# Attention scores in split precision: three one-pass products for a pair of heads in the two row halves

## The reference

```python
# gqa: each query block of 128 sees the key blocks n-1, n, n+1
scores = jnp.einsum("bnqhgd,bnkhd->bnhgqk", qb, kw).astype(jnp.float32) * (d ** -0.5)
# na: rows of a 16 x 64 grid, a window of 8 rows x 16 columns, learned bias
scores = jnp.einsum("brqhd,brikhd->brhqik", qg, kg).astype(jnp.float32) * (d ** -0.5)
# dif: causal, two maps j of a head, bias slope_h * (k - q), p0 - lambda * p1
s = jnp.einsum('bqhjd,bkhjd->bhjqk', qb, kb).astype(jnp.float32) * scale
```

## Time and profile before

| | |
|---|---|
| median of 3 runs | 3774.08 us (3770.61 to 3774.63) |
| profiled execution: span from first to last instruction | 3768.5 us |
| its own time beside the span | not given apart; the median is 5.6 us above the span |
| mean granted TensorE clock | 0.986 of full speed |
| busy: TensorE, weight load, VectorE, ScalarE, GpSimd | 3636.0, 2873.4, 1829.1, 704.6, 1308.4 us |
| window attention (first layer) | 125.9 to 275 us |
| neighbourhood attention (first layer) | 436 to 550 us |
| differential attention (first layer) | 1556.8 to 1692 us |

### The profile page before, as it was taken

One profiled execution on the slowest core, in us unless ns is written; L12 is line 12 of the kernel. 1 busy time (PEld: TensorE's weight loads), 2 busy tenths in 40 slices (PEclk: granted clock), 3 DMA queues, 4 the chain that ended last, 5 costly groups with the idle time before them and its releaser, 6 DMA issues.

```text
span 3768.5 us, 44735 instructions
## 1 busy us (share of the span) xinstructions
PE 3636.0 (96%) x16872; PEld 2873.4 (76%) x16872; DVE 1829.1 (49%) x2567; ACT 704.6 (19%) x1417; POOL 1308.4 (35%) x549
## 2 busy tenths in 40 slices
PE   8999999999998999999999999999998999999997
PEld 6777667777766788667888888888875788888886
DVE  5667536568536424576432422451447654143146
ACT  2220232120134000363100100110025411000002
POOL 3324203323303333203443444553220244444443
PEclk9999999999999999999999999999999999999998
DMA  3101202111201111101111111111110011111112
GB/s 130 40 29 40 53 12 62 51 29 34 64 12 34 34 51 34 56 1 40 45 50 50 45 50 50 50 57 50 37 59 7 29 45 47 48 50 50 45 50 73
DMA packets 60995, 168.98 MB, mean 45 GB/s; under 512 B 20640, under 2 KB 21024, under 8 KB 60832
## 3 DMA queue, kind: packets, MB, share of 16 engines
q1 hardware_dynamic: 39168, 142.62, 12.1%
q10 hardware_dynamic: 21664, 24.19, 2.2%
HBM read 159.45 MB, written 4.19 MB: 43 GB/s over the span
## 4 chain that ended last, share of the span: by engine, by line
PE 65%; DVE 3%; issue 2%; ACT 1%; DVEq 0%; ACTq 0%
PE ps L455 57%; PE ps L516 3%; PE ps L562 2%; PE ps L545 1%; DVE in_lo L1094 0%; DVE space_hi L1192 0%; PE ps L482 0%; PE ps L725 0%; ACT st L862 0%; DVE st L1103 0%; PE ps L721 0%; PE ps L573 0%; DVE st L1129 0%; PE ps L493 0%; PE ps L707 0%
## 5 line engine op out<-in xcount | busy, mean ns | idle before, releaser
L398 POOL TENSOR_TENSOR w_hi<-w_raw,ones 128x1024 fp32r<-128x1024 f32 x272 | 531.2, 1953 | 2398.5 <-PE ps L455 2394.4
L455 PE MATMUL ps<-in_hi,w_hi 128*128 128x512 f32 x3584 | 1138.2, 399 | 54.0 <-DVE in_lo L1094 21.7
L455 PE MATMUL ps<-in_hi,w_lo 128*128 128x512 f32 x3584 | 1116.3, 393 | 0.0
L455 PE MATMUL ps<-in_lo,w_hi 128*128 128x512 f32 x3584 | 1115.0, 392 | 0.0
L455 PEld LDWEIGHTS ps<-in_hi,w_hi 128*128 128x128 f32 x3584 | 661.2, 189 | 214.5 <-DVE in_lo L1094 26.7
L455 PEld LDWEIGHTS ps<-in_hi,w_lo 128*128 128x128 f32 x3584 | 671.9, 189 | 152.9 <-issue 13.4
L455 PEld LDWEIGHTS ps<-in_lo,w_hi 128*128 128x128 f32 x3584 | 674.4, 189 | 146.4 <-issue 4.4
L402 POOL TENSOR_TENSOR w_lo<-w_raw,w_hi 128x1024 fp32r<-128x1024 f32 x272 | 776.8, 2856 | 21.3
L1079 DVE TENSOR_TENSOR st<-ps,rfac 128x1024 f32<-128x1024 f32 x148 | 181.1, 1224 | 757.8 <-PE ps L455 726.5
L1085 DVE TENSOR_TENSOR xt<-xt,ps 128x1024 f32<-128x1024 f32 x112 | 136.7, 1221 | 413.3 <-PE ps L455 411.0
L516 PE MATMUL ps<-st 64*128 64x384 f32 (+3 forms) x704 | 250.0, 535 | 9.2 <-DVE small L1192 9.1
(11 more groups left out here) (147 smaller groups left out, 2598.4 us busy)
## 6 DMA issues: line engine op xcount, KB each, us to landing
w_raw<-w_in SPq DMA_DIRECT2D x272, 512.0 KB, 3.5
xt<-x_in ACTq DMA_DIRECT2D x8, 512.0 KB, 8.9
space_lo<-c_alibi ACTq DMA_DIRECT2D x2, 2048.0 KB, 8.0
out<-xt ACTq DMA_DIRECT2D x8, 512.0 KB, 3.0
st<-st ACTq DMA_DIRECT2D x24, 128.0 KB, 2.7
st<-c_rope ACTq DMA_DIRECT2D x2, 1024.0 KB
space_lo<-rpb_in ACTq DMA_DIRECT2D x2, 960.0 KB, 7.3
space_lo<-rpb_in ACTq DMA_DIRECT2D x2, 944.0 KB, 12.3
```

The lines of the kernel that those rows point to most:

```text
L398: pool.tensor_tensor(w_hi[:, j, :], w_raw[:, j, :], ones[:, 0:1].broadcast_to([P, KC * P]), ALU.mult).then_inc(pool_own, 1)
L455: last = pe.matmul(ps[:, 2 * j + h, :], w[:, w_slot, (w_k + k) * P:(w_k + k + 1) * P], part[:, k0 + k, h * HALF:(h + 1) * HALF], start=(k ...
```

## The change

Every score product becomes three products of fp32r operands, as in the projections: `q_hi*k_hi + q_lo*k_hi + q_hi*k_lo`. They are issued for two heads (in dif for the two maps of a head) in turn, one in rows 0 to 63 into bank 4, the other in rows 64 to 127 into bank 5. In gqa and na, heads t and t+1 are scored together: step `u` (even) issues the first piece of both, step `u+1` the second piece, if there is one, and the scores stand at the end of the step. A pair waits until VectorE is done with both pieces of the pair before it.

The parts have to be made: ScalarE copies the keys and the queries of each round to fp32r (`key_hi`, `query_hi`), VectorE subtracts (`key_lo`, `query_lo`); the queries of two rounds are made ahead of the attention and the others during it, in a ring of two. Their places in gqa are the last two chunks of the residual `xt`, which a DMA of 1 MB writes out to DRAM at the layer's beginning and another brings back after the attention. In dif, one ALiBi table (0.5 MB) takes the place of four (2 MB), with the slope moved to the scale of VectorE's operation and a power of two per head into the evacuation of the queries. In gqa and na, ScalarE's exponentials move behind its copy of the second group.

```diff
+                    if t == 0 and i == 0:
+                        pe.wait_ge(qk_lo.handle, qk_lo.at(stack, l, split_index(kind, n)))
...
                     for piece in pieces_of(tiles_of_round(kind, n))[i:i + 1]:
-                        for j in range(maps):
-                            q, base = query(t, j)
-                            p = state["p"]
-                            if p >= 2:
-
-                                pe.wait_ge(biased.handle, biased.at(stack, l, p0 + p - 1))
-                            pe.matmul(ps[:, 4 + p % 2, 0:len(piece) * P],
-                                      q[base:base + HD, n * P:(n + 1) * P],
-                                      key(t, j)[base:base + HD, piece[0] * P:(piece[-1] + 1) * P],
-                                      start=True, stop=True).then_inc(scored.handle, 1)
-                            state["p"] += 1
+                        p = state["p"]
+                        if p >= 2:
+
+                            pe.wait_ge(biased.handle, biased.at(stack, l, p0 + p))
+                        cols = slice(piece[0] * P, (piece[-1] + 1) * P)
+                        for q, k in ((q_hi, k_hi), (q_lo, k_hi), (q_hi, k_lo)):
+                            for j in range(2):
+                                rows = slice(HD * j, HD * (j + 1))
+                                last = pe.matmul(ps[:, 4 + j, 0:len(piece) * P], q[rows, c, :], k[rows, cols],
+                                                 start=(q is q_hi and k is k_hi), stop=(k is k_lo))
+                                if k is k_lo:
+                                    last.then_inc(scored.handle, 1)
+                        state["p"] += 2
...
+            def key_hi(stack, l, kind, c):
+
+                source, hi, _ = key_parts(kind, c)
+                act.activation(hi, source, ACT.Copy).then_inc(qk_hi.handle, 1)
+
+            def query_hi(stack, l, kind, n, p0=0):
+
+                if n >= 2:
+
+                    act.wait_ge(scored.handle, scored.at(stack, l, p0 + pieces_before(kind, n - 1)))
+                source, hi, _ = query_parts(kind, n)
+                act.activation(hi, source, ACT.Copy).then_inc(qk_hi.handle, 1)
...
+                    if kind != "dif" and 3 <= u < len(units) + 3:
+                        groups(u - 3, 1)
                     if 1 <= u < len(units) + 1:
                         exps(u - 1)
-                    if 3 <= u < len(units) + 3:
+                    if kind == "dif" and 3 <= u < len(units) + 3:
                         groups(u - 3, 1)
+                    if u % 4 == 1 and 2 <= u // 4 + 1 < NB:
+                        query_hi(stack, l, kind, u // 4 + 1, p0)
...
+                act.dma_start(x_kept, xt[:, KC - KEPT:KC, :]).then_inc(x_put.handle, 16)
...
                 act.wait_ge(done.handle, done.at(1, l, 24))
-                act.dma_start(space_lo[:, :, :], c_alibi.rearrange("h p n -> p h n")).then_inc(alibi_in.handle, 16)
+                act.dma_start(space_lo[:, 0, :], c_alibi).then_inc(alibi_in.handle, 16)
+                query_hi(1, l, "dif", 0)
+                query_hi(1, l, "dif", 1)
...
+            def query_lo(stack, l, kind, n):
+
+                source, hi, lo = query_parts(kind, n)
+                dve.wait_ge(qk_hi.handle, qk_hi.at(stack, l, split_index(kind, n)))
+                dve.tensor_tensor(lo, source, hi.bitcast(F32), ALU.subtract).then_inc(qk_lo.handle, 1)
...
+                    if u % 4 == 2 and 2 <= u // 4 + 1 < NB:
+                        query_lo(stack, l, kind, u // 4 + 1)
...
+                key_lo(0, l, "gqa", 0, 1)
+                query_lo(0, l, "gqa", 0)
+                query_lo(0, l, "gqa", 1)
...
                 dve.wait_ge(lo_ready.handle, lo_ready.at(1, l, 4))
-                steps = attention(1, l, "dif", 0, 0, 0, lambda n, t: space_lo[:, t, S - (n + 1) * P:S], None)
+                query_lo(1, l, "dif", 0)
+                query_lo(1, l, "dif", 1)
+                key_lo(1, l, "dif", 3, 4 + 2)
+                steps = attention(1, l, "dif", 0, 0, 0, lambda n, t: space_lo[:, 0, S - (n + 1) * P:S], None)
```

More of the change, by code:

```diff
@@ L127, in products_done, with pieces_before @@
     return i + 1 if i < first else min(first + 2 * (i - first + 1), first + KC + i - first + 1)
+def pieces_before(kind, n):
+    lanes = 2 if kind == "dif" else 1
+    return sum(4 * lanes * len(pieces_of(tiles_of_round(kind, m))) for m in range(n))
 STEPS = 4 * NB + 8
@@ L495, in turn_values, with attention @@
                     last.then_inc(vt_ready.handle, 1)
-            def attention(stack, l, kind, p0, g0, r0, query, key, value, width):
+            def attention(stack, l, kind, p0, g0, r0, value, width):
                 maps = 2 if kind == "dif" else 1
@@ L590, in step @@
                     if u < len(units):
-                        scores(u, 1)
+                        if kind == "dif":
+                            scores(u, 1)
+                        else:
+                            scores(u - u % 2, u % 2)
                 return [lambda u=u: step(u) for u in range(STEPS)]
@@ L977, in _ @@
                                    ).then_inc(lnact_ready.handle, 1)
+                for c in range(2):
+                    act.wait_ge(taken.handle, taken.at(0, l, 24 + c + 1))
+                    key_hi(0, l, "na", c)
                 act.wait_ge(conv_out.handle, conv_out.at(0, l, 2))
@@ L1027, in _ @@
                     last.then_inc(r_squared.handle, 1)
+                act.wait_ge(taken.handle, taken.at(1, l, 19))
+                for c in range(3):
+                    key_hi(1, l, "dif", c)
                 for c in (0, 1, 2):
@@ L1173, in scores @@
                     for piece in pieces_of(tiles)[i:i + 1]:
-                        for j in range(maps):
-                            m = maps * u + j
-                            i = maps * t + j
-                            first = cur[:, C_SINK + t:C_SINK + t + 1] if kind == "gqa" else 3.0e38
+                        for j in range(2):
+                            m = 2 * u + j if kind == "dif" else u + j
+                            i = 2 * t + j if kind == "dif" else t + j
+                            first = cur[:, C_SINK + i:C_SINK + i + 1] if kind == "gqa" else 3.0e38
                             dve.wait_ge(scored.handle, scored.at(stack, l, p0 + state["p"] + 1))
@@ L1248, in step @@
                         mix(u - 2)
-                    if u < len(units):
+                    if u < len(units) and kind == "dif":
                         scores(u, 0)
@@ L1454, in _ @@
                 add_to_x(0, l, 28, 0)
+                for c in range(2):
+                    key_lo(0, l, "na", c, 1 + NB + c + 1)
+                query_lo(0, l, "na", 0)
+                query_lo(0, l, "na", 1)
                 dve.wait_ge(bias_in.handle, bias_in.at(0, l, 64))
@@ L1587, in _ @@
                         r_next(n - 1)
-                    evacuate(1, l, 12 + n, st[:, places[n], :])
+                    if n < 4:
+                        dve.wait_ge(done.handle, done.at(1, l, 12 + n + 1))
+                        dve.scalar_tensor_tensor(st[:, places[n], :], flat(ps, 2 * (n % 2), 2), 2.0 ** (2 * (n + 1)), rfac[:, :],
+                                                 ALU.mult, ALU.mult).then_inc(taken.handle, 1)
+                    else:
+                        evacuate(1, l, 12 + n, st[:, places[n], :])
                     if n < NB:
@@ L1695, in constants @@
     r = np.arange(S)[None, :] - (S - P) - np.arange(P)[:, None]
-    alibi = np.stack([np.where(r <= 0, 2.0 ** (-2.0 * (h + 1)) * r / SCALE, NEG / SCALE) for h in range(4)])
+    alibi = np.where(r <= 0, r / SCALE, NEG / SCALE)
     return {"c_ident": eye, "c_rope": rope, "c_gqa": gqa, "c_na": na, "c_ret": ret, "c_alibi": alibi}
```

86 lines of the change are left out of this document (67 added, 19 removed).

## The result

The changed kernel takes 3748.16 us against 3773.41 for the kernel before: ratio 0.9934, 95% interval [0.9918, 0.9949]. The median is that of four executions: three took 3745.11 to 3751.18 us, the fourth 9033.1, which the ratio leaves out; its cause is not known. A second batch gave 3750.74 us and 0.9948 [0.9932, 0.9965]. It is faster, as forecast, but by 25 us (20 in the second batch) instead of 78, and outside the range of 3668 to 3739.

A forecast was written before the change was run, and what follows sets the result against it. TensorE's own stream was taken as the bound. Window and neighbourhood attentions save 90.4 us, less 8 for waits (82), less 4 lost in the differential attention: 78; 3768.5 - 78 + 5.6 = 3696 us, range 3668 to 3739.

The forecast's parts named there:

- The pair's price: Scores of two heads, halves running together: 0.38, 0.55, 0.72, 0.89 us for 128, 256, 384, 512 keys.
- (a): Rival, score pairs: each weight load shows, 37 us given back, 3733 us; chance 0.14.
- (c): Rival, score pairs: the row halves take turns, 12 us lost, 3786 us; chance 0.05.
- The window attention: Score blocks there: four become two in each round, saving 17.5 us a layer.
- The neighbourhood attention: Score blocks there: four become two in each round, saving 27.7 us a layer, late copies costing 3.
- The 8 us that I took off 90.4: Window and neighbourhood attentions, both layers: allowance for waits and late copies, leaving 82 us of gain.
- The differential attention: That stage: 1.7 us gained less 3.8 at its entry, 2.1 us lost a layer, 4 in all.
- the entry's term for VectorE's two subtractions: Differential entry: first scores wait for two subtractions of 0.69 us behind an addition, 2.6 us a layer.
- one more microsecond or two: Differential entry: more idling may keep TensorE at its lower clock that much longer; left to the range.
- The 4.1 us of query subtractions: Differential attention, VectorE: six subtractions of 0.69 us a layer, not covered, set against the pairs' gain.
- the 5.8 of gain: Differential attention: cheaper pairs save 1.6 us in rounds 0 to 3 and 4.2 in rounds 4 to 7, per layer.
- (b): Rival, window and neighbourhood attentions: waits for both banks and between engines take the gain, 3739 us; chance 0.13.

The follow-up runs named there:

- experiment 1: Changed kernel with window and neighbourhood scores issued again between the transposes and what follows them: 3750.64 us, ratio 0.9954 to the kernel before.
- experiment 3: Changed kernel with VectorE's first two query subtractions and a key subtraction of the differential attention moved ahead of projection 25's addition: 3726.67 us, ratio 0.9896.
- experiment 7: On experiment 3, differential query parts of rounds 2 to 7 left out, output not the reference's: 3723.42 us, ratio 0.9876.
- experiment 8: Changed kernel with differential scores back at plain fp32, there waiting for both banks before the first map's products: 3722.26 us, ratio 0.9877.

## Why the prediction was wrong, by its own steps

**The pair's price: right.** 0.72 and 0.89 us, in the products' order and head by head. Rivals (a) and (c) fall with it: (a) wanted 0.93 us for 384 keys, (c) 1.24. The rule of the Trainium skill (TensorE: Matmul & The Clock Gate, Part 3: Packing small matmuls) that a weight load overlaps only with products of another row group is not borne out where a half loads again behind its own product: three loads a half add nothing to 0.72. What was wrong beside it is a phrase: the "third of the work" that the differential stage saves is, by the prices next to it, 0.171 us per 128 keys in place of 0.21, a fifth.

**The window attention: the cover failed, not the size.** Of 17.5 us a layer 13.4 came in the first. In the kernel before, a score block stood between three transposes and the transposes back, and I counted only its own time and the 0.20 us for the insertion. It was also the cover for ScalarE's copy. Moved to the end of the step it covers nothing: 0.58 us of wait in a round. With the products with the values in that place, 17.9 us came. I had allowed 1 us for the attention.

**The neighbourhood attention: the same step failed.** 27.7 less 3 were forecast and 17.0 came. In a round of five tiles 1.7 us instead of 4.1: waits take 1.66, and experiment 1, which puts the cover back, has none of them and saves 3.4 (16.86 - 13.44). Some 0.7 are left, about what I had counted for four insertions fewer (4 x 0.20); whether it is that term, no run isolates. The forecast had late copies ("a copy can be late by some 0.2 us"), at 0.8 us a round, and ScalarE's two waits do come to 0.93, but its reason was ScalarE's order of work, where experiment 1 shows the lost cover. The third wait, 0.73 us for VectorE's heads, had no term. The 8 us that I took off 90.4 for both attentions should have been 90.4 - 55.7 = 35. The second layer of this kind gained 25.3 us and the first 30.4; what makes the difference was not followed, and the second execution of the changed kernel has 27.7 in the first and 25.4 in the second.

**The differential attention: wrong by 26 us.** The step that failed is the entry's term for VectorE's two subtractions. It stood at 2.6 us a layer of the entry's 3.8 and took 9.6 (19.2 of span for two, experiment 3). The rest of the entry, 1.2 us for ScalarE's copies, comes to 0.7. The order of the queue was right: two subtractions stood in front of all TensorE work. Their duration was not. Mine, 0.69 us, was the row of an operation while GpSimd was idle; here the pair ended at 1502.54 + 4.09 = 1506.63, just after GpSimd's split of the weights (1503.41 + 2.67 = 1506.08). The first of the two took 1.35 us and ended at 1503.89, in the same way just after GpSimd's operation before that (1501.44 + 1.89 = 1503.33): each ends some 0.55 us behind one of GpSimd's, so most of its own 0.69 came after it. The Trainium skill (SBUF — State Buffer, SBUF: two separate sides) states that a VectorE operation with two inputs in SBUF and a GpSimd operation that reads SBUF lock each other out for a whole instruction; the trace agrees, 4.09 us beside it and 1.29 without. The rule was there to be looked up, and GpSimd's order of time at that point belonged to the step. Then the clock: I had "one more microsecond or two"; it was 14 us at the lower level where there had been none, which by experiment 3 is a consequence of the wait.

Some 5 us a layer are lost beside that, where 1.7 of gain and ScalarE's 1.2 had been forecast. The 4.1 us of query subtractions don't show (experiment 7), and neither does the 5.8 of gain: under the shared wait for both banks the shorter pair takes as long as the fp32 one (experiments 3 and 8). The shared wait itself costs 7.2 us for two layers, measured on fp32 products (experiment 8). The prediction names this wait only in the 8 us off the other two attentions, and in rival (b); in the differential sum it stood at nothing. The reading that time saved on TensorE hardly shows in this stage was right, and the sum took the 5.8 us in full all the same. That it costs the split products the same is an inference: a wait for each half alone wasn't tried.

The 5.6 us between span and median held by luck (5.0 after). An execution takes some 2 us more than its own span (3745.11 and 3743.2); the rest was spread between executions, since the span lies only 2.1 us below the fastest of the three (3770.61).

**What it was, of the rivals.** (b) came nearest: it named waits in place of work, and 3739; the time is past it because the entry came on top. But it put the waits for both banks in the window and neighbourhood attentions, and there they are 1.5 us a layer; what cost time there was the missing cover. They lie in the differential attention, where (b) had nothing.

## What to carry to other kernels

A block of TensorE work that is moved or shortened has two prices: its own time, and what it covered. Look at what stands directly behind it and which engine that waits for, before you move it; and put another independent block in its place. Before an operation is put on VectorE in front of a TensorE wait, see what GpSimd does in just that stretch. And where two products share one wait, the wait is for the slower: 7 us here with no other change. A shorter product behind such a wait may then gain nothing.

## What the runs showed of the hardware that was not expected

- Two subtractions of 512 columns took 4.09 us while GpSimd split weights, 1.29 us while it was idle. The second alone took 2.82 us, and each ended some 0.55 us behind one of GpSimd's operations.
- Three one-pass products in each row half take 0.72 us for 384 columns, whether the halves are issued in turn or one after the other (0.73). So the halves overlap however they are queued.
- A wait of 5.32 us was followed by some 14 us at the lower level; one of 3.07 us by some 4 (the products are back at 0.62 us from 1493.01); waits of 1.38 and 1.78 us by 3.4 us each. Behind a wait of 0.58 us the products have the same length as elsewhere (0.78 us for the six at 195.48 and at 203.87).
